# Two planner weights of the expert-choice part raised, from 21 to 26 and from 23 to 30

## The reference

```python
q = (h @ w_q).reshape(bn, sn, PEER_HEADS, 2, PEER_DQ // 2)
scores = jnp.einsum('bshpd,hpnd->bshpn', q, sub_keys).astype(jnp.float32)
s, i = lax.top_k(scores, PEER_TOPK)
...
top_s, pos = lax.top_k(cand_s, PEER_TOPK)
idx = jnp.take_along_axis(cand_i, pos, axis=-1)
gate = jax.nn.softmax(top_s, axis=-1)
...
u = jnp.take(expert_u, it, axis=0)
a = jax.nn.gelu(jnp.einsum('tkd,td->tk', u, ht).astype(jnp.float32), approximate=False) * gt
vv = jnp.take(expert_v, it, axis=0)
return jnp.einsum('tk,tkd->td', a.astype(vv.dtype), vv)
```

## Time and profile before

| | |
|---|---|
| median of three executions | 3494.28 us (3481.57 to 3499.15) |
| the profiled execution | 3481.57 us |
| span from its first to its last instruction | 3479.8 us |
| TensorE, VectorE, ScalarE, GpSimd busy | 80%, 68%, 33%, 34% of the span |
| bytes moved by DMA, mean rate | 1247.28 MB, 358 GB/s |
| first and last dot product (`L1480`) | 390.7 us and 3460.4 us |

### The profile page before, as it was taken

One profiled execution on the slowest core, in us unless ns is written; L12 is line 12 of the kernel. 1 busy time (PEld: TensorE's weight loads), 2 busy tenths in 40 slices (PEclk: granted clock), 3 DMA queues, 4 the chain that ended last, 5 costly groups with the idle time before them and its releaser, 6 DMA issues. The chain is left out here.

```text
span 3479.8 us, 29554 instructions
## 1 busy us (share of the span) xinstructions
PE 2772.3 (80%) x8472; PEld 1532.6 (44%) x8472; DVE 2350.4 (68%) x5514; ACT 1163.8 (33%) x3409; POOL 1171.6 (34%) x1065
## 2 busy tenths in 40 slices
PE   3787788798979768886898769887799777777776
PEld 2565443465555426544444337444455322233222
DVE  6775888637868965676588954776679954445544
ACT  1131233327822232372233322574223322322222
POOL 0000244312223232333444433333344443343332
PEclk9857899999989988978999989978999999999999
DMA  7663799968899799999999999989999999999997
GB/s 270 253 238 116 284 420 416 391 248 291 287 338 369 273 362 380 398 356 353 420 419 410 415 401 381 361 325 351 361 419 411 394 397 421 419 411 407 422 421 330
DMA packets 272766, 1247.28 MB, mean 358 GB/s; under 512 B 19925, under 2 KB 114517, under 8 KB 141399
## 3 DMA queue, kind: packets, MB, share of 16 engines
q0 software_dynamic: 153792, 1098.97, 78.6%
q1 hardware_dynamic: 118802, 146.35, 11.9%
q10 hardware_dynamic: 8, 0.06, 0.0%
HBM read 1243.18 MB, written 7.36 MB: 359 GB/s over the span
## 5 line engine op out<-in xcount | busy, mean ns | idle before, releaser
L1421 PE MATMUL psum<-space 128*128 128x512 f32 x3484 | 1727.7, 634 | 445.7 <-ACT space L1454 391.2
L1528 POOL DMA_INDIRECT space<-in_peer_uv,expert x1024 | 1153.5, 1126 | 2025.7 <-PE psum L1421 1436.2
L1480 DVE CUSTOM_DVE_ANT_0 space<-space,h 128x1024 f32<-128x1024 f32 x1024 | 1248.4, 1223 | 799.1 <-DMA space<-in_peer_uv,expert 729.5
L1421 PEld LDWEIGHTS psum<-space 128*128 128x128 f32 x3484 | 663.0, 200 | 1260.1 <-issue 608.2
L1443 ACT ACTIVATE space<-space 128x2 f32<-128x2 f32 x512 | 103.9, 203 | 1596.9 <-DVE space L1480 1595.4
L594 PE MATMUL psum<-space 128*128 128x256 f32 (+2 forms) x1840 | 440.4, 398 | 88.9 <-DMA space<-in_w_out_c 31.2
L594 PEld LDWEIGHTS psum<-space 128*128 128x128 f32 x1840 | 362.0, 200 | 187.1 <-issue 72.0
L1454 ACT ACTIVATE space<-ident,space 128x128 f32<-128x128 f32 x871 | 302.7, 386 | 1.0 <-PE psum L1421 1.0
L1115 PE MATMUL psum<-space 128*128 128x256 f32 x1024 | 261.3, 383 | 11.7 <-ACTq L460 11.7
L1115 PEld LDWEIGHTS psum<-space 128*128 128x128 f32 x1024 | 195.8, 193 | 140.2 <-issue 110.8
L1446 ACT ACTIVATE space<-space,gate 128x1 f32<-128x1 f32 x1024 | 245.5, 286 | 16.8
(11 more groups left out here) (163 smaller groups left out, 1714.4 us busy)
## 6 DMA issues: line engine op xcount, KB each, us to landing
space<-in_peer_w_q SPq DMA_DIRECT2D x32, 1024.0 KB
space<-in_ada_w SPq DMA_DIRECT2D x12, 2048.0 KB, 15.8
space<-in_ada_w POOLq DMA_DIRECT2D x12, 2048.0 KB, 9.4
space<-in_w_in_c SPq DMA_DIRECT2D x24, 1024.0 KB
space<-in_peer_uv,expert POOLq DMA_INDIRECT x1024
space<-in_w_in_ab SPq DMA_DIRECT2D x14, 1024.0 KB
space<-in_w_out_ab SPq DMA_DIRECT2D x8, 1024.0 KB
space<-skewed SPq DMA_DIRECT2D x32, 256.0 KB
```

The costliest lines, as they stand in the source:

```text
L1421: last = nc.tensor.matmul(b.bank[part][:, :], b.diag2[:, n % DIAGS, :], b.pairs[:, p % PAIRS, 1, part * BANK:(part + 1) * BANK], start=(p ...
L1480: dve.tensor_tensor_reduce(out=row, in0=row, in1=b.h[:, tile(q), :], scale=1.0, scalar=0.0, op0=ALU.mult, op1=ALU.add, accum_out=b.dots2[: ...
L1528: pool.indirect_dma_start(out=b.pair_rows[q % PAIRS], out_offset=None, in_=ins["peer_uv"], in_offset=bass.IndirectOffsetOnAxis(ap=b.expert ...
```

## The change

The cost that `choice_part` lists per head is raised from 21.0 to 26.0 for the second half in layer 0 and from 23.0 to 30.0 for both halves in layer 1. No instruction's form changes; the planner's list and the windows of `Sums` follow from the new costs.

```diff
-                    choice_part(nc, ins, b, kit, 1, half, s_chosen, 23.0)]
+                    choice_part(nc, ins, b, kit, 1, half, s_chosen, 30.0)]
...
-            phases = [layer0_parts(1) + [choice_part(nc, ins, b, kit, 0, 1, s_chosen, 21.0, rows=(0, 5))],
+            phases = [layer0_parts(1) + [choice_part(nc, ins, b, kit, 0, 1, s_chosen, 26.0, rows=(0, 5))],
```

## The result

The changed kernel takes 3504.78 us (median of 20 executions, 3488.86 to 3526.61); the kernel before 3487.63 us (median of 20, 3476.94 to 3504.65). The ratio is 1.0052 with a 95% interval of 1.0035 to 1.0068, so +18 us, between +12 and +24. The forecast was +25, added to a median of three executions that lay 7 us above this median of twenty, so of the 14 us between 3519 and 3505 half is the starting point and half the change. The profiled execution of the changed kernel took 3502.65 us, its span 3500.9 us.

The account below looks back on a forecast made before the run. DMA was taken to bound layer 1's choice stages and the last stretch, VectorE phase 0's choice. Phases 1, 2 and 0 gave 14 + 10 + 1 = +25 us, so 3494 + 25 = 3519 us, range 3504 to 3539.

Parts of the forecast that it names:

- the stages ahead: Stages before the choice: fewer picks save 26 us in phase 1, 31 in phase 2, 8 in phase 0.
- DMA's price: Choice stages of layer 1: each added pick costs 2.53 us, sixteen more per phase, 81 us together.
- VectorE's price: Choice of phase 0: each added pick costs 1.3 us (dot product and accumulator read), 9 us for seven.
- VectorE's account: Attention of layer 1: 1.95 us per pick, saving 10 us in phase 1 and 14 in phase 2.
- rival 2: Stages ahead follow DMA, 2.53 us per pick there too; phases 1 and 2 even, 3485 to 3494 us; 22%.
- The 1.0: Transposes, output product and norm ahead of the choice: 1.0 us per pick, saving 4 and 3 us.
- The 1.7 and 1.5: Norm and product ahead of the choice: us per pick in phases 1 and 2, saving 12 and 9 us.
- The 2.3: Norm and product: us per pick between phases 1 and 2, before taking off weight waits and clock.
- The flush of the fifth tile: Output product of phase 2: TensorE's 8.4 us flush wait moves into the choice, counted as 5 us saved.
- The windows: VectorE's windows end earlier, so it adds 133 v rows instead of 153; TensorE takes the other 20.
- Rival 1: Picks ahead of the choice cost only TensorE's 0.78 us everywhere: +60 us, so 3554; 10%.
- Rival 3: Picks ahead cost their stage's mean (3.30, 3.44, 4.13 us): -28 or -46 us, so 3448 to 3466; 18%.

Follow-up runs that it names:

- the single run of this part: Only the layer 0 weight raised (26, 23, 23) against the kernel before: ratio 0.9999 (0.9984 to 1.0015), about 0 us.
- oldwin: The changed kernel with VectorE's windows of before, leaving the 20 v rows with VectorE: ratio 1.0050 to the kernel before, about +17 us.
- its single run: Only the weight of layer 1's second half raised (21, 23, 30) against the kernel before: ratio 0.9999 (0.9979 to 1.0020), about 0 us.
- p1_paired: Weights 21, 30, 23 with phase 1's attention ticks moved from even picks to the odd pick behind them: ratio 1.0016 to the kernel before.
- unpair1: The kernel before with one tick per pick in phase 1's attention, instead of two behind odd picks: ratio 1.0020 (0.9994 to 1.0045).

## Why the prediction came out, and where it did not

The direction, the size and the sums of the stages were right; the prices inside the stages ahead were not. Attention was to give back 24 us in layer 1 and gave 4, the other parts were to give 33 and gave 60, and by luck the two errors largely cancelled. The means below are over the traces with the same plan in the phase and ticks as the planner laid them (in the choice stages over all traces with the same weight there).

- **The choice stages of layer 1 pay DMA's price.** Forecast +40 and +41 us. Measured 328.4 to 372.3 us in phase 1 and 295.8 to 337.7 us in phase 2: +44 and +42. The step was right, 2.6 to 2.8 us per pick instead of 2.53.
- **The choice of phase 0 pays VectorE's price.** Forecast +9; measured 214.6 to 223.6 us, +9. The stage ahead: forecast -8, measured 380.7 to 372.2 us, -8.5. Even, and the single run of this part agrees. That VectorE is what sets the price there rests on the size alone, and `oldwin` speaks rather against it at the start of the stage.
- **The stages ahead in layer 1.** Forecast -26 and -31. Measured 391.6 to 362.2 us and 445.1 to 410.6 us: -29 and -34. The sums were right to 3 us.
- **What failed is their make-up.** I priced attention at VectorE's account, 1.95 us per pick, so -10 in phase 1 and -14 in phase 2. Measured: 112.8 to 114.2 us in phase 1, that is +1, and 179.2 to 174.3 us in phase 2, -5, where single traces of each plan spread by 9 to 16 us. The account assumed that the ticks would lie between the picks as well as they had before; in phase 1 they did not, since the share of 1.898 had made pairs of them and 2.195 broke these. Without pairs ScalarE and TensorE wait for each other. That is a little over half of the miss in phase 1: with pairs the two traces took 108.0 and 107.0 us, so even then five picks gave only 5 us, 1.1 each and not 1.95. Why VectorE's account is too high there stays open.
- **The other parts paid more than I gave them.** I priced norm, product, transposes and output at 1.0 to 1.7 us per pick. Measured, attention taken off: 278.8 to 248.0 us in phase 1, 2.8 us for each of eleven picks by the plan (2.6 for twelve by the gathers), and 265.9 to 236.3 in phase 2. There rival 2 (DMA's price on both sides) was right. The 1.0 came from one comparison of phase 1 with phase 2 in one execution, 101.6 against 103.3 us, and 8.4 us of the second were the flush of a finished tile, which the first hadn't; without it the fall is 6.7 us for four picks, 1.7 each. The 1.7 and 1.5 rest on a wrong sum: at a granted clock of 0.90 a fifth of 172.1 us is at the lower level, 34.4 us and not 17.2, and at 0.94 it is 19.0 of 158.1 and not 9.5, so 0.6 us per pick would have been left and not 1.2. The 2.3 of the rows as they stood, with nothing taken off, lay nearest to what was measured.
- **The flush of the fifth tile** did leave the output product of phase 2, and in the choice TensorE waits 3.2 us for it instead of 8.4, a difference of 5, as I had counted. The piece from the end of attention to the end of the stage went from 108.50 to 91.90 us with three gathers fewer; the same piece of phase 1, which had no flush, went from 105.10 to 90.80 with five fewer.
- **The windows.** No price was put on the 20 v rows, and `oldwin` shows none.
- **The rivals.** Rival 1 (TensorE's price everywhere, +60) did not come. Rival 2 (0 to -9 in all) did not either: in attention the picks didn't pay DMA's price. Rival 3 (the stage's mean per pick) did not come for the change, but a price near its own (3.3) was met in the other direction: from 23 to 18, fifteen picks cost the stage ahead of phase 1 435.40 - 391.6 = 44 us, 3.0 each, of which 18 us come back in attention with pairs (134.50 against 116.40 us).

What stays open: by the sums above phase 2 should cost 7 us, and its single run says 0, between -7 and +7; the first stands at the edge of the second, and nothing here separates them. Whether pairs explain the whole of phase 1's +17 us is also not settled. `p1_paired` brought it to +6 (-3 to +14); of those 11 us the attention's 6 are seen in the traces, and the rest is within what executions differ by. Why the attention of phase 0 does not gain from pairs wasn't tried. And what TensorE's clock adds of itself isn't known: in phase 2 the attention of one and the same plan took 170.1 us at a granted clock of 0.94 and 186.3 at 0.84.

## What to carry to other kernels

A plan by costs fixes more than how much work stands beside each transfer: it also fixes behind which step of a loop over several engines each piece falls, and here that was worth more than the change of shares (with the weight 18, pairs turned +22 us into -15, where the change costs 18). Before reading the effect of a changed share as a price, print the pattern that the plan makes, and compare kernels with the same pattern. And moving picks out of a stage on DMA's ceiling into one beneath it pays only while the first stays on the ceiling: the gain at 18 was gone at 14.

## What the runs showed of the hardware

ScalarE changed its table twice per round in the attention, once for gelu (L1453) and once for the attention's own function (L907). In the timeline of `unpair1` above the load starts at 1532.49, 0.01 us after the copy before it ended (1532.09 + 0.39), takes 1.28 us, and the gelu starts 0.02 us after it. The Trainium skill's page "ScalarE: Activation LUTs", section "What ACT_TABLE_LOAD costs", gives about 1283 ns for the load, which agrees, and a drain of about 1380 ns beside it, which these rows don't show.
